# A product-key router's matmuls placed between the weighted sums of an expert stage

## What is computed

```python
q = (xb @ wq).reshape(PEER_BLOCK, PEER_HEADS, 2, PEER_DKEY // 2)      # 8 heads, 2 halves of 128
s = jnp.einsum('thpd,pkd->thpk', q, subkeys)                           # scores against 2 x 128 keys
s1, i1 = lax.top_k(s[:, :, 0], 16);  s2, i2 = lax.top_k(s[:, :, 1], 16)
cand = s1[..., :, None] + s2[..., None, :]                             # 256 candidates
top_s, sel = lax.top_k(cand, 16);  idx = ...                           # 16 experts of a head
g = softmax(top_s)
act = gelu(einsum('thkd,td->thk', u_tab[idx], xb))                     # 128 experts of a token
y = einsum('thk,thkd->td', g * act, v_tab[idx])
```

## Time and profile before

| | |
|---|---|
| runs of the kernel before | 2360.61 us median of 3 (2357.73 to 2371.1) |
| the profiled execution | 2363.29 us; its span, first to last instruction, 2361.6 us |
| TensorE matmul busy | 1784.2 us (76%) |
| VectorE busy | 1206.1 us (51%) |
| GpSimd busy | 1088.3 us (46%) |
| ScalarE busy | 512.3 us (22%) |
| mean granted TensorE clock | 0.863 |

### The profile page before, as it was taken

The page is one execution under the profiler, slowest core; times in us unless marked ns, Lnnn a source line. Parts: engine busy times, 40 slices in busy tenths (PEclk is TensorE's granted clock), DMA queues, the critical chain, the costliest instruction groups (busy, mean ns, idle before and its releaser), DMA issues.

```text
span 2361.6 us, 22167 instructions
## 1 busy us (share of the span) xinstructions
PE 1784.2 (76%) x4939; PEld 871.1 (37%) x4939; DVE 1206.1 (51%) x3154; ACT 512.3 (22%) x1265; POOL 1088.3 (46%) x1308
## 2 busy tenths in 40 slices
PE   6989889797467676767677667777766777778766
PEld 2434455253323333333333333333333333444422
DVE  2222232213645655546555544656554577867773
ACT  1212223111111222212222211221221132322231
POOL 2000000000365655656566565666655566666554
PEclk8989999876688888988888898878888898899889
DMA  7866636332999898999898898999989999998877
GB/s 276 321 231 237 213 137 241 120 108 68 345 363 332 321 329 312 351 343 351 315 333 327 322 346 325 346 326 328 332 323 334 330 359 336 359 350 324 327 293 278
DMA packets 228617, 703.41 MB, mean 298 GB/s; under 512 B 22910, under 2 KB 40416, under 8 KB 228529
## 3 DMA queue, kind: packets, MB, share of 16 engines
q0 software_dynamic: 156672, 570.49, 65.6%
q1 hardware_dynamic: 71560, 131.03, 16.0%
q10 hardware_dynamic: 312, 1.07, 0.1%
HBM read 694.72 MB, written 8.25 MB: 298 GB/s over the span
## 4 chain that ended last, share of the span: by engine, by line
issue 27%; DVE 26%; another core or an unknown queue 6%; PE 5%; ACT 5%; DMA 3%; DVEq 1%; POOL 1%; ACTq 0%; SPq 0%; POOLq 0%
DVE u_rows L1701 14%; PE ps_y L1906 4%; DMA u_rows<-in_peer_u_dram,u_idx 2%; ACT wt_diag L1624 2%; DVE key_scores_w L1712 1%; DVE top_i L1714 1%; DVE top_i L1715 1%; DVEq L57 1%; DVE top L1713 1%; DVE top L1711 1%; ACT L1649 1%; DVE cand_w L1712 1%; DVE one_hot L1737 1%; DVE one_hot L1741 1%
## 5 line engine op out<-in xcount | busy, mean ns | idle before, releaser
L1906 PE MATMUL ps_y<-v_rows,wt_diag 128*128 128x512 f32 x2176 | 1094.2, 659 | 195.8 <-ACT wt_diag L1624 122.9
L1906 PEld LDWEIGHTS ps_y<-v_rows,wt_diag 128*128 128x128 f32 x2176 | 452.4, 214 | 763.3 <-issue 730.5
L1542 POOL DMA_INDIRECT u_rows<-in_peer_u_dram,u_idx x544 | 519.8, 956 | 409.7 <-DVE dots L1701 173.7
L1701 DVE CUSTOM_DVE_ANT_0 u_rows<-u_rows,ps_h_cur 128x1024 f32<-128x1024 f32 x544 | 633.8, 1217 | 90.0 <-DMA u_rows<-in_peer_u_dram,u_idx 67.6
L1542 POOL DMA_INDIRECT v_rows<-in_peer_v_dram,v_idx x544 | 511.1, 939 | 235.5 <-issue 159.6
L1711 DVE MAX8 top<-key_scores 128x8 f32<-128x128 f32 x80 | 22.8, 285 | 444.0 <-issue 263.3
L370 PE MATMUL ps_z<-w_stream,hT 128*128 128x512 f32 (+5 forms) x560 | 233.8, 573 | 16.7 <-DVE hT L529 16.7
L1890 PE MATMUL ps_r<-ident,q 128*128 128x128 f32 x80 | 23.7, 393 | 256.1 <-ACT q L1609 237.4
L625 POOL TENSOR_TENSOR z_cc_ch<-z_cc_ch 128x256 f32<-128x256 f32 (+1 forms) x5 | 3.6, 723 | 376.0 <-DVE z_cc_ch L566 376.0
L1882 PE MATMUL ps_r<-wq,hT_next 128*128 128x256 f32 (+1 forms) x640 | 157.8, 403 | 23.4 <-issue 14.4
L1624 ACT ACTIVATE wt_diag<-ident,wts 128x128 f32<-128x128 f32 x544 | 166.3, 388 | 38.3 <-DVE wts L1707 20.7
(11 more groups left out here) (372 smaller groups left out, 1339.2 us busy)
## 6 DMA issues: line engine op xcount, KB each, us to landing
w_stream<-in_w_in_dram SPq DMA_DIRECT2D x25, 2048.0 KB, 7.9
w_stream<-in_ada_w_dram SPq DMA_DIRECT2D x12, 2048.0 KB, 13.0
u_rows<-in_peer_u_dram,u_idx POOLq DMA_INDIRECT x544
v_rows<-in_peer_v_dram,v_idx POOLq DMA_INDIRECT x544
wq<-in_peer_wq_dram SPq DMA_DIRECT2D x4, 2048.0 KB, 18.3
w_stream<-in_w_in_dram SPq DMA_DIRECT2D x5, 1568.0 KB, 7.9
w_stream<-in_w_in_dram SPq DMA_DIRECT2D x5, 1536.0 KB, 6.4
w_out<-in_w_out_dram SPq DMA_DIRECT2D x1, 4096.0 KB, 18.4
```

The lines of the kernel that those rows point to most:

```text
L1542: g.indirect_dma_start(rows[:, j, :], None, table, bass.IndirectOffsetOnAxis(where[:, j:j + 1], 0))\
L1701: v.tensor_tensor_reduce(u_rows[:, j, :], u_rows[:, j, :], h_cur[:, :], 1.0, 0.0, ALU.mult, ALU.add, dots[:, par, j:j + 1]).then_inc(s["u_ ...
L1906: mm = nc.tensor.matmul(ps_y[:, c * 512:(c + 1) * 512], diag[:, par, j, :], v_rows[:, j, c * 512:(c + 1) * 512], start=(first and j == 0), ...
```

## The change

On TensorE, a head's queries are moved from ahead of a group's sums to behind the sums of slots 0 and 1, the transposes from behind slot 1 to behind slot 3, and the scores from behind slot 3 to behind slot 5. The scores are written to columns 256 to 511 of bank 1, beside the transposes, and no longer beside the queries in bank 0; with that the wait for the copy of the last head's scores (`sc_out`) moves from the queries to the transposes. ScalarE reads the scores from the new place. Nothing else differs: no instruction is added or removed.

```diff
@@ ScalarE, head
-                    a(sc[:, :, :], ps_r[:, 0, 256:512], ACT.Copy).then_inc(s["sc_out"], 1)
+                    a(sc[:, :, :], ps_r[:, 1, 256:512], ACT.Copy).then_inc(s["sc_out"], 1)
@@ TensorE
                 def head_q(H, h):
 
-                    if not isinstance(H, int) or H:
-                        hold(pe, s["sc_out"], H)
                     for kc in range(KC):
...
                 def head_qT(H):
 
                     hold(pe, s["q_out"], H + 1)
+                    if not isinstance(H, int) or H:
+                        hold(pe, s["sc_out"], H)
                     for k in range(2):
...
-                        mm = nc.tensor.matmul(ps_r[:, 0, 256 + k * PK:256 + (k + 1) * PK], qT[:, k, :], subT[:, k, :], start=True, stop=True)
+                        mm = nc.tensor.matmul(ps_r[:, 1, 256 + k * PK:256 + (k + 1) * PK], qT[:, k, :], subT[:, k, :], start=True, stop=True)
...
                     if rows is not None:
                         rows_t(rows)
-                    if keys is not None:
-                        head_q(keys, h)
                     if new_tile is not None:
                         hold(pe, s["y_out"], new_tile)
                     sums(i, par, range(0, 2), first)
                     if keys is not None:
-                        head_qT(keys)
+                        head_q(keys, h)
                     sums(i, par, range(2, 4))
                     if keys is not None:
+                        head_qT(keys)
+                    sums(i, par, range(4, 6))
+                    if keys is not None:
                         head_scores(keys)
-                    sums(i, par, range(4, NB))
+                    sums(i, par, range(6, NB))
```

## The result

The changed kernel took 2549.6 us (median of 3, 2547.83 to 2550.91) against 2360.61: ratio 1.0791, 95% interval 1.0754 to 1.0827, slower by 189 us, where 2370 had been forecast with a range to 2440. The span of its profiled execution is 2547.9 us against 2361.6. TensorE's busy time rose from 1784.2 to 1808.8 us only, and the DMA engines are less full.

A forecast was written before the change was run, and what follows sets the result against it. The chain of a pair, about 51 us, was taken as the bound, through the gather-held release of the queries' copy. Terms -11 - 11 + 32 = +10 us on 2363.29 gave 2373, by the median 2370; range 2315 to 2440.

The forecast's parts named there:

- What bounds the kernel: Expert stage: a pair's chain of scores, routing, dots, diagonals sets about 51 us; inside it, when the queries' copy is released.
- The gathers of the burst depend on none of it, so the release stays at 1262.7: Loop pairs: the moved matmuls leave the burst's end alone, so the queries' copy starts when it did; no added time.
- 22 held heads: Loop heads whose queries' copy waits for the gather burst to drain: 0.5 us gained each, -11 us, bounds 0 and -42.
- The gap of 4.1 us and the 5.4 us for two slots behind it: Loop pairs: TensorE's idle time before the transposes shrinks from 10.2 to about 4.1 us; two slots then take about 5.37.
- The second pairs, +21: Three heads where a tile's second pair begins: queries lose the cover of the diagonals' wait, 6.9 us each, 21 together.
- The last tile, -11 for nine heads and +11 for three: Last tile: nine held heads gain 11 us (bounds 0 and -20); three not held lose 5.2 and about 3 each, 11.
- The bank, the wait for `sc_out`, the first pair at nothing: Scores' new bank, moved wait for their last copy, and first pair, whose v rows land slot by slot: no cost.
- Rival 1: Loops and last tile: the count is late by a fixed time after the queries' matmuls; +134, near 2510; chance 0.07.
- free heads: Six heads not held, three in tiles' second pairs and three in the last tile: +32 us, bounds +20 and +90.
- Rival 2: TensorE's clock stays up after the 4.1 us gap: -42 and -20 in place of -22, 2331 us; chance 0.20.
- Rival 3: Loops: sums behind the queries let their count out at once, so no hold: -147, 2235 us; chance 0.12.
- Rival 4: The six free heads become held, as queries fall 7 us deeper into the burst: +60 more, 2430; chance 0.19.

The follow-up runs named there:

- cut-back burst: Changed kernel, but GpSimd's v gathers of slots 0 and 1 wait for slot 2's count, which stands behind the queries: 2404.11 us, 1.018.
- j - 2: GpSimd issues the u gather of slot j only when u rows of two slots before have landed: 1.0111 on the kernel before, 1.0182 on the changed one.
- looser settings: Kernel before, u gathers paced by landings two or three slots back, in all groups or odd ones only: ratios 0.9773 to 1.0111.
- j - 1: Kernel before, with the u gather of slot j waiting until the u rows of the slot just before have landed: 3392.2 us, one run.

## Why the prediction was wrong, by its own steps

- **What bounds the kernel**: right. The chain of a pair goes through the copy of the queries, and that copy follows the gathers and not the queries. The cut-back burst shows it (5.49 us behind the v gather, with the queries 6 us later in the group than before), and with the bursts gone all 22 copies of the loops are prompt.
- **"The gathers of the burst depend on none of it, so the release stays at 1262.7"**: this is the step that failed. The gathers of the sixteen depend on none of it; where the burst ends depends on `v_used` of slot 0, which the prediction itself had listed as late, and the change moves exactly the counts of slots 0 and 1 ahead of the late stretch. The prediction looked at the counts of slots 2 and 3, found that their gathers wait in order behind slot 0's, and did not ask what slot 0's own gather would do. The -11 us of the 22 held heads became +129: the release is 5.6 us later in the mean (20.9 against 15.3), and 22 times that is 123. The forecast's own sign of failure, a copy later than 5.5 us behind the burst's last v gather, is what came.
- **The gap of 4.1 us and the 5.4 us for two slots behind it**: right, when the burst ends where it was thought to. With the burst cut back TensorE is, in the pair shown, idle for 4.21 us ahead of the transposes, and the two slots behind them take 5.37 us; over the 22 heads the gap goes from 0 to 5.6 us. The held heads then give -6 us, within the bounds of 0 and -42 and smaller than the 11 taken.
- **The second pairs, +21**: right, +20 (and 54.1 - 34.7 = 19.4 with the burst cut back).
- **The last tile, -11 for nine heads and +11 for three**: mis-sized, +38 and, with the burst cut back, +21. The step took the two first slots at 3.46 us, warm. But with the queries behind them TensorE has nothing to do ahead of the diagonals, there as in the tiles' second pairs, and starts cold, on the slow clock. From the timeline of the changed kernel's last tile:

```profile
2310.90 5.50 PE L1906 MATMUL ps_y<-v_rows,wt_diag 128*128 128x512 f32 x8 [7.32 <-ACT wt_diag L1624]
2316.24 3.62 PE L1880 MATMUL ps_r<-wq,hT_next 128*128 128x256 f32 x16
2319.69 3.60 PE L1906 MATMUL ps_y<-v_rows,wt_diag 128*128 128x512 f32 x8
```

  Two cold slots (5.34 us from start to start), the queries (3.45 us) and twice two warm slots (3.45 us each time) are 15.7 us, and with the transposes, the scores and the copies between some 17 to 20 us from the diagonals to VectorE, in a place where the kernel before needed 10.7 to 22.8 us, 16.7 in the mean. Eight of the twelve copies come within 0.4 us of the queries' end, so it is mostly TensorE's own time.
- **The bank, the wait for `sc_out`, the first pair at nothing**: right for the first two (1.0008); the first pair costs 8 us.
- **Rival 1**, the hold that follows the queries, gave 2510 and came nearest in time, for another reason (its own terms, 134 and the 32 of the free heads, already make 2527 without the last tile's nine). Its mechanism, a fixed delay, is refuted: 7.7 to 13.9 us in one kernel and 2.1 to 8.3 us with the burst cut back. **Rival 2** didn't come: the two slots behind the 9.79 us gap take 6.37 us, where they took 6.36. **Rival 3**, no hold, didn't come. **Rival 4** didn't either: the copies of all six free heads come within 0.2 us of the queries' end.

With the burst cut back the four classes measured add up to -6 + 19 + 21 + 5 = +40 us, and the time went up by 2404.11 - 2365.57 = 39. The forecast's terms for the same classes give +10. So the failed step is worth 139 us, four gathers in each burst, and some 29 us more are sizes: 21 in the last tile, 5 in the first pair, 5 in the held heads.

What stays open is the mechanism of the hold itself. Shown is that it comes with gathers issued without regard to their landings and is gone when they are paced to j - 2, that it can touch each of the router's counts and `v_used`, and that in the loops of the two unpaced kernels it ends 2.5 to 3.5 us behind the start of the burst's last gather (1.2 us in two heads). The traces also stamp the semaphore events from which the releasers are inferred, and these tell where the delay lies. In all 22 heads of the loops, the only event of the queries' count is stamped 6.4 to 14.8 us behind the modelled end of their matmuls in the kernel before, 7.7 to 13.8 us in the changed one, and less than 0.1 us ahead of the copy. With pacing (j - 2) it is stamped 0.01 to 0.02 us behind that end, in the 37 of 44 heads where it was recorded. In the pair of the earlier trace rows the event of the queries stands at 1262.62, those of slots 0 and 1 at 1262.67 and 1262.73, though the matmuls ended 1.7 us apart. So it is in 20 of the 22 heads; in the other two slots 0 and 1 come 1.5 us behind the queries. "Remote", then, is TensorE's own count: the event itself is late and not ScalarE's view of it, and the late counts come out in their order within some 0.1 us, like a queue that is let go. Whether the depth of what is under way or the full rate does it, no run here tells. The Trainium skill, "Perfetto Trace Analysis", section "Tensor Engine Instruction (MATMUL, LD_WEIGHTS)", says that the profiler estimates a matmul's end, while its count goes out only when PSUM has acknowledged the write; that leaves room for a late count behind a matmul that looks done. The late events lie in that room, and what fills it these traces don't show. The matmuls that follow start at their usual distance (3.45 us for two slots) while the count is out, so TensorE's array isn't what is held.

## What to carry to other kernels

When a wait is let go by something that the profile can't name, find what it keeps a constant distance to, and then ask which waits end *that*; a change that moves a semaphore ahead of a stall can lengthen the burst that causes the stall. A matmul that fills a wait for another engine is free where it is, and costs its full time behind the wait; in the last tile here a cold start came on top. Where long bursts of gathers run beside a chain of short steps between engines, try pacing the gathers by landings before reordering the chain: on the kernel before, this gave from 0.9773 to 1.0111 at the looser settings and 1.42 times the time at the tightest, and the reorderings gave between 0.9927 and 1.0791.

## What the hardware showed that was not expected

- Counts of TensorE's come up to 15 us behind the end of their matmuls, under 1.02 of DMA share in gathers, and their semaphore events are stamped as late; with gathers paced to 0.92, wherever ScalarE stands waiting for the queries, it starts 0.1 us behind their end. The Trainium skill, "SBUF — State Buffer", section "Who interferes with whom", says that a DMA never contends with a compute engine and that TensorE and ScalarE wait for nobody. The durations of their instructions agree (3.60 to 3.67 us for two warm slots with bursts and without), and the rule is about ports; the handing over between them, which it doesn't speak of, is what suffers here.
- The even stream costs little rate: 324 GB/s against 335 in the mean of the stage, and the granted clock rises from 0.86 to 0.96, with TensorE no longer idle for 10 us ahead of the transposes.
- A gather of 128 rows of 4 KB takes 4.3 us from issue to landing in the median with two or three under way (the run at j - 1). At 2.5 us a slot, a wait for the landing of two slots before already binds: the run at j - 2 has the gathers on the chain that ended last.
